# One front stage for modulation and norm, a deferred modulation on GpSimd, and decay and gate rows over 128 partitions

## What is computed

```
m_lat = split(silu(c)     @ w_mod + b_mod, 6)     # shift1, scale1, gate1, shift2, scale2, gate2
m_ctx = split(silu(c_ctx) @ w_mod + b_mod, 6)     # of these only shift1, scale1 are used
h     = rms_norm(x, norm1_g) * (1 + scale1) + shift1      # latent and context tokens
p     = h @ w_in                                  # 4640 columns: q k v ga | 32 decay and gate columns | hq hff hfb hv gb
log_g = -exp(a_log) * softplus(p_a + dt_bias);  beta = sigmoid(p_b)      # from the 32 columns
... two scans (gated delta rule, HGRN2), each forward and backward, w_out ...
x     = x + gate1 * y
x     = x + gate2 * mlp(rms_norm(x, norm2_g) * (1 + scale2) + shift2)
```

## Time and profile before

| | us |
|---|---|
| median of three runs | 4352.18 |
| the profiled execution, its own time | 4353.56 |
| its span, first to last instruction | 4351.8 |
| TensorE busy | 3614.9 |
| VectorE busy | 1880.8 |
| ScalarE busy | 1377.6 |
| POOL busy | 697.0 |
| mean granted TensorE clock | 0.907 |

### The profile page before, as it was taken

How to read it: one execution, slowest core, us unless ns; L and a number is a source line. 1 busy time by engine, 2 the same in 40 slices (tenths; PEclk the granted TensorE clock), 3 DMA queues, 4 the chain that set the end, 5 groups by cost and what they waited for, 6 DMA issues and landing times. The chain is left out here.

```text
span 4351.8 us, 98698 instructions
## 1 busy us (share of the span) xinstructions
PE 3614.9 (83%) x42292; PEld 2976.9 (68%) x42292; DVE 1880.8 (43%) x2660; ACT 1377.6 (32%) x1858; POOL 697.0 (16%) x752
## 2 busy tenths in 40 slices
PE   2549999999968888857674428899999888999998
PEld 2327788888857777747664227688888666888886
DVE  7647851111025555545546943523323335233233
ACT  0336641433125555513332212312212223122122
POOL 0000000000035555505556102000000220000002
PEclk9779999999979999966777668899999888999998
DMA  6412232243223333354442263111111231111111
GB/s 234 145 43 49 54 80 75 99 130 100 72 95 109 108 106 113 104 105 85 102 86 70 68 217 107 35 48 52 44 52 46 81 107 35 49 52 44 52 46 58
DMA packets 460370, 365.08 MB, mean 84 GB/s; under 512 B 115908, under 2 KB 413192, under 8 KB 454408
## 3 DMA queue, kind: packets, MB, share of 16 engines
q1 hardware_dynamic: 430088, 315.94, 25.2%
q0 software_dynamic: 6912, 25.17, 1.7%
q10 hardware_dynamic: 23168, 20.97, 1.6%
HBM read 262.64 MB, written 99.39 MB: 83 GB/s over the span
## 5 line engine op out<-in xcount | busy, mean ns | idle before, releaser
L2289 PE MATMUL o_pg<-o_h_hi,o_w_hi 128*128 128x512 f32 x1280 | 516.9, 404 | 70.6 <-DVE o_h_lo L2438 48.6
L527 PE MATMUL p_pg<-h_hi,p_whi 128*128 128x512 f32 (+3 forms) x1384 | 531.4, 384 | 25.5 <-DVE p_wlo L702 25.5
L527 PE MATMUL p_pg<-h_lo,p_whi 128*128 128x512 f32 (+3 forms) x1384 | 519.3, 375 | 0.0
L527 PE MATMUL p_pg<-h_hi,p_wlo 128*128 128x512 f32 (+3 forms) x1384 | 519.3, 375 | 0.0
L2290 PE MATMUL o_pg<-o_h_lo,o_w_hi 128*128 128x512 f32 x1280 | 509.1, 398 | 0.0
L2291 PE MATMUL o_pg<-o_h_hi,o_w_lo 128*128 128x512 f32 x1280 | 509.0, 398 | 0.0
L2289 PE MATMUL o_pg<-o_f_hi,o_w_hi 128*128 128x512 f32 x1024 | 398.3, 389 | 0.0
L2290 PE MATMUL o_pg<-o_f_lo,o_w_hi 128*128 128x512 f32 x1024 | 398.3, 389 | 0.0
L2291 PE MATMUL o_pg<-o_f_hi,o_w_lo 128*128 128x512 f32 x1024 | 398.3, 389 | 0.0
L2289 PEld LDWEIGHTS o_pg<-o_h_hi,o_w_hi 128*128 128x128 f32 x1280 | 245.6, 192 | 150.8 <-issue 46.9
L527 PEld LDWEIGHTS p_pg<-h_hi,p_whi 128*128 128x128 f32 (+1 forms) x1384 | 258.4, 187 | 81.5 <-DVE p_wlo L702 26.3
(11 more groups left out here) (279 smaller groups left out, 6265.6 us busy)
## 6 DMA issues: line engine op xcount, KB each, us to landing
o_raw<-in_w_mlp SPq DMA_DIRECT2D x128, 512.0 KB, 4.1
g_kqvb<-scr_kqv SPq DMA_DIRECT2D x72, 384.0 KB, 3.5
mod_w<-in_w_mod SPq DMA_DIRECT2D x6, 4096.0 KB, 13.1
p_raw<-in_w_in SPq DMA_DIRECT2D x38, 512.0 KB, 5.9
g_kqa<-scr_kqv SPq DMA_DIRECT2D x72, 256.0 KB, 3.0
scr_kqv<-p_y SPq DMA_DIRECT2D x24, 576.0 KB, 4.9
scr_hf<-p_y SPq DMA_DIRECT2D x16, 576.0 KB, 5.3
scr_hk<-p_s SPq DMA_DIRECT2D x16, 576.0 KB, 8.2
```

Source lines behind the costliest of these rows:

```text
L527: last = nc.tensor.matmul(pg[0:m, bank, 0:n], w[:, q, k, 0:m], h[:, k, hoff:hoff + n], start=(k == 0 and j == 0), stop=(k == KT - 1 and j ...
L2289: nc.tensor.matmul(out, w_hi[:, p, k, :], half(rhs[0], k, h), start=(k == 0), stop=False)
```

## The change

`phase_mod` and `phase_norm` become one `phase_front`, and parts of `phase_project` change.

- **Front.** Only the first 2048 of the 6144 columns of w_mod are used here, in eight slices of 1 MB (one per row group) through four slots. TensorE multiplies them directly, with silu(c) and silu(c_ctx) as two stationary columns (`products`); the result is two rows, turned by 16 small transposes. The small vectors are loaded from ScalarE's queue, decay constants from POOL's in 16 transfers.
- Squares are taken from the tokens before the transpose, per tile of 128 tokens with an accumulated sum: three tiles of a block on ScalarE, the fourth on VectorE. The sums are thus one number per partition; the reciprocal is of 128 x 4, becomes four diagonal matrices, and a matmul with ones spreads it (`spread`).
- The scaled row is one VectorE operation (gain and reciprocal root together), `h_hi` adds the shift on ScalarE, and `h_lo` is one VectorE operation (add the shift, subtract `h_hi`).
- Token loads, stores of xT (now from SP's queue) and the first two weight tiles of the projection stand in one written-out order; x has two buffers, some of the buffers lie in space of later `h` blocks. `h_hi` and `h_lo` are one tensor per block.
- **Projection.** The 32 decay and gate columns are repeated four times, so the result stands on 128 partitions; each 32 partitions keep one latent block and a quarter of the context (576 elements). All four rows live in `p_y1`. They are stored in 32 transfers; only tile 1 waits for them. No step in the scans' arithmetic changes.
- **Deferred modulation.** POOL multiplies and adds the other 4096 columns of w_mod in eight pieces of 512 columns, 64 slices of 256 KB that it loads itself, and TensorE sums each piece over the partitions after every fourth tile. `e.mod` and the last gain are finished at the end of the projection.

```
+def phase_front(nc, e):
...
+                for k in range(4):
+                    load_w(k)
+                load_x(0)
+                for k in range(4, KT):
+                    load_w(k)
+                load_x(1)
+                load_x(2)
+                sp.dma_start(e.p_raw[:, 0, :, 0:AB_W], e.w_in[0].rearrange("(k p) n -> p k n", p=P)[:, :, AB_COL:AB_COL + AB_W]
+                             ).then_inc(e.p_w_in[0], 16)
+                sp.dma_start(e.p_raw[:, 1], e.w_in[0].rearrange("(k p) n -> p k n", p=P)[:, :, 0:P]).then_inc(e.p_w_in[1], 16)
+                store(1)
+                load_x(3)
+                store(2)
+                load_x(4)
+                store(3)
+                store(4)
+                for i in range(3):
+                    sp.wait_ge(stored[i], 16 * len([q for q in range(2, 10) if q % 3 == i]))
...
+                def products(k):
+                    pe.wait_ge(wm_in[k % 4], 16 * (k // 4 + 1))
+                    for n in range(4):
+                        last = nc.tensor.matmul(mp[0:2, n, :], e.sc[:, k, :], wm[k % 4][:, n, :],
+                                                start=(k == 0), stop=(k == KT - 1))
+                    last.then_inc(wm_used, 1)
...
+                for b in range(1 + NB):
+                    for k in range(KT + 1):
+                        if k < KT:
+                            copy(b, k)
+                        if k >= 1:
+                            high(b, k - 1)
+                        if 1 <= b < NB and 3 <= k < 6:
+                            square(b + 1, k - 3)
+                        if 1 <= b < NB and k == 6:
+                            roots(b + 1)
...
+                    dve.scalar_tensor_tensor(ur[:, g % UR, 0:n], xt[:, g % RING, 0:n], e.gain[:, g0 + k:g0 + k + 1],
+                                             mp[:, b % 2, 0:n], ALU.mult, ALU.mult).then_inc(u_ready, 1)
...
+                    dve.scalar_tensor_tensor(e.h_lo[b][:, k, :], ur[:, g % UR, 0:n], e.mod[:, s0 + k:s0 + k + 1],
+                                             e.h_hi[b][:, k, :].bitcast(F32), ALU.add, ALU.subtract).then_inc(lo_ready, 1)
...
+                def mod_sums(c, released):
+                    pe.wait_ge(m_acc, c + 1)
+                    pe.wait_ge(group_free, released)
+                    for s in range(TB // P):
+                        last = nc.tensor.matmul(modps[:, c * 4 + s:c * 4 + s + 1], macc[:, s * P:(s + 1) * P],
+                                                e.ones[:, 0:1], start=True, stop=True)
+                    last.then_inc(m_sums, 1)
...
+                for x in range(MC * KT):
+                    c, k = divmod(x, KT)
+                    w = mw[:, x % 2]
+                    sc = e.sc[:, k, 0:1]
+                    pool.wait_ge(mw_in[x % 2], 16 * (x // 2 + 1))
+                    if k == 0:
+                        if c:
+                            pool.wait_ge(m_sums, c)
+                        nc.gpsimd.tensor_scalar(macc[:, :], w, sc, None, ALU.mult).then_inc(m_part, 1)
+                        done += 1
+                    else:
+                        nc.gpsimd.tensor_scalar(w, w, sc, None, ALU.mult).then_inc(m_part, 1)
+                        pool.wait_ge(m_part, done + 1)
+                        nc.gpsimd.tensor_tensor(macc[:, :], macc[:, :], w, ALU.add).then_inc(m_part, 1)
+                        done += 2
...
+                nc.scalar.activation(whi[:, 0].rearrange("p k (q r) -> p k q r", q=4),
+                                     raw[:, 0, :, 0:AB_W].unsqueeze(2).to_broadcast([P, KT, 4, AB_W]), ACT.Copy).then_inc(w_hi, 1)
...
+                        nc.scalar.activation(ab_g[r, to], src, ACT.Identity, bias=e.dtb[r, :])
+                        last = nc.scalar.activation(ab_y[r, to], src, ACT.Sigmoid)
...
-                        if m < 2:
-                            act.wait_ge(ab_out, 16 * 6)
-                        else:
+                        if m == 1:
+                            act.wait_ge(ab_out, 16 * 32)
+                        elif m:
...
-                dve.wait_ge(ab_out, 16 * 3)
-                dve.tensor_tensor_scan(yrow[0][0:AB_W, :], m, g, 0.0, ALU.mult, ALU.add).then_inc(ab_d, 1)
+                dve.tensor_tensor_scan(ab_c, m, g, 0.0, ALU.mult, ALU.add).then_inc(ab_d, 1)
```

More of the change, by code:

```diff
@@ L128, in _ @@
+            @block.scalar
+            def _(act):
                 v = [(V_BMOD, 48, e.b_mod[0].rearrange("(r n) -> r n", n=P)),
@@ L140, in _ @@
[L140 to L149, removed]
@@ new lines, in high @@
+                def high(b, k):
+                    g = 8 * b + k
+                    nt, g0, s0 = BLOCKS[b]
+                    act.wait_ge(u_ready, g + 1)
+                    nc.scalar.activation(e.h_hi[b][:, k, :], ur[:, g % UR, 0:nt * P], ACT.Identity,
+                                         bias=e.mod[:, s0 + k:s0 + k + 1]).then_inc(hi_ready, 1)
+                for a in range(2):
+                    square(0, a)
+                roots(0)
+                for a in range(3):
+                    square(1, a)
@@ new lines, in inverse @@
+                def inverse(b):
+                    t, n = T0[b], BLOCKS[b][0]
+                    dve.wait_ge(root, b + 1)
+                    dve.reciprocal(rs[:, t:t + n], rs[:, t:t + n]).then_inc(inv, 1)
+                    dve.wait_ge(inv, b + 1)
+                    if b:
+                        dve.wait_ge(bc_ready, b)
+                    for a in range(n):
+                        last = dve.tensor_scalar(diag[:, a, :], e.ident, rs[:, t + a:t + a + 1], None, ALU.mult)
+                    last.then_inc(diag_ready, 1)
@@ new lines, in _ @@
+                dve.tensor_copy(mrow[:, 2:4, :], mp[0:2, 2:4, :]).then_inc(mrow_dve, 1)
+                dve.wait_ge(mod_turned, 1)
+                m = cc[:, C_MOD:C_MOD + 32].rearrange("p (s a) -> p a s", a=2)
+                bm = e.cols[:, V_BMOD:V_BMOD + 16]
+                dve.tensor_tensor(e.mod[:, 0:16], m[:, 0, :], bm, ALU.add).then_inc(chain, 1)
+                dve.tensor_tensor(e.mod[:, 48:64], m[:, 1, :], bm, ALU.add).then_inc(chain, 1)
+                dve.wait_ge(chain, 7)
+                for j, sc0 in enumerate((8, 56)):
+                    last = dve.scalar_tensor_tensor(e.gain[:, 8 * j:8 * j + 8], e.mod[:, sc0:sc0 + 8], 1.0,
+                                                    e.cols[:, V_G1:V_G1 + 8], ALU.add, ALU.mult)
@@ new lines, in _ @@
+                last.then_inc(mod_ready, 1)
+                dve.wait_ge(mod_ready, 1)
+                for b in range(1 + NB):
+                    for k in range(KT + 1):
+                        if k < KT:
+                            scale(b, k)
+                        if k >= 1:
+                            low(b, k - 1)
+                        if b == 0 and k == 2:
+                            inverse(1)
+                        if 1 <= b < NB and k == 4:
+                            square(b + 1)
+                        if 1 <= b < NB and k == 7:
+                            inverse(b + 1)
@@ L400, in phase_project @@
         pgf = pg[:, :, :].rearrange("p b t -> p (b t)")
+        AL = TB + CTX // 4
+        ab_y, ab_g, ab_m, ab_c = (yrow[1][:, x * AL:(x + 1) * AL] for x in range(4))
         def group_no(m, j):
@@ L484, in store @@
+                load(0)
+                sp.wait_ge(ab_a, 5)
+                for d in range(2):
+                    store_ab(e.sbeta[d], 16 + 8 * d, ab_y, d)
+                sp.wait_ge(ab_d, 6)
+                store_ab(e.sgam[0], 0, ab_c, 0)
+                sp.wait_ge(ab_d, 9)
+                store_ab(e.sgam[1], 8, ab_g, 1)
                 def store(m):
```

478 lines of the change are left out of this document (251 added, 227 removed).

## The result

| | before | after |
|---|---|---|
| median of the runs beside each other, us | 4355.73 | 4186.98 |
| lowest to highest of four | 4346.83 to 4361.99 | 4185.07 to 4188.69 |
| ratio after to before, 95% interval | | 0.9614, 0.9594 to 0.9633 |
| span of the profiled execution, us | 4351.8 | 4183.2 |

The change gives 168.7 us, and 168.6 between the two profiled spans.

A forecast was written before the change was run, and what follows sets the result against it. TensorE matmuls bound most of the kernel (83% busy), but not its first 345 us. Gains of 140.8 (front) and 18.8 (decay rows), less 14.3 and 2, made 143.3 off 4353.6, then 1.4 less: 4209 us, range 4193 to 4232.

The forecast's parts named there:

- Shift and gain at 40.3: New front: products to 34.8 us, then copies, small transposes and VectorE's sums, so shift and gain stand at 40.3 us.
- 2 us, twice: Front's latent blocks: ScalarE, and VectorE behind it, wait 2 us twice for token tiles queued behind stores; 112.6 becomes 116.6.
- Rival A: Front: transfers set its length, ScalarE's squares waiting 8 us in three blocks and a late last store; +20, 4229; chance 0.15.
- Rival D: Front: steps at the engines' floor, 1.25 us each, and no transfer wait; -13, 4196; chance 0.12.
- First sums at P+41.9 and idle 6: Projection: first sums of squares 41.9 us after its first matmul, against 60.7 before, TensorE idle 6 before them; 18.8 gained.
- Rival E: Decay rows: the hole in the projection stays, as the 128-partition chain or its many stores take as long; 4228; chance 0.02.
- 1.78 per piece, 14.3 lost: Deferred modulation in the projection: TensorE's fp32 column sums cost 1.78 us for each of eight pieces, 14.3 us lost.
- I give the products 2.4 GHz: Start of the front: modulation products run at 2.4 GHz, 32 x 0.86 = 27.5 us; a slow start would cost 2 us.
- Rival C: Front: modulation products run at 1.2 GHz throughout; +27, 4236; chance 0.05.
- VectorE beside POOL, 2 us: Projection: POOL's deferred modulation lengthens VectorE operations with SBUF inputs; between 0 and 7.8 us, taken as 2 lost.
- Rival B: Projection: POOL's collisions reach further, stretching 39 normalising multiplications after 345 us by 0.4 and splits as much; +18, 4227; chance 0.07.
- rival F: Projection: TensorE waits every four tiles for POOL's piece; slower than before, 4414 at 17 us a slice; chance 0.01.

## Why the prediction was wrong, and where it was right

The order of things came as forecast: the front gives nearly everything, the decay rows 19, the deferred sums take a little back, nothing else moves. Nearly all the errors went the same way, so together they left the range.

- **The front, 122.5 forecast and 111.69 measured.** Shift and gain at 40.3: 40.34. In it two errors cancel. The products ran to 37.26 and not 34.8, for the most part because TensorE started at 1.2 GHz (2.2 of the 2.5); the 16 small transposes took 1.1 us and not 3.5. I priced them by a row that differs twice: it turned 128 columns where these have two, and its stretch, 165 to 169 us, has a granted clock of 0.57. Then the context block took 8.2 (9.7 forecast), the three blocks 47.6 (49.5), the last 11.6 (11.6). Inside a block errors cancel as well. In block 2, five plain steps took 6.7 (7.25 forecast) and the three with squares 6.0 (7.2), but the change to the next block took 3.3 and not 2.0, as these two scalings show, 4.63 apart of which 1.3 is the step:

```profile
75.56 0.74 DVE L398 SCALAR_TENSOR_TENSOR n_u<-n_xt,gain,n_mp 128x512 f32<-128x512 f32 x1
80.19 0.75 DVE L398 SCALAR_TENSOR_TENSOR n_u<-n_xt,gain,n_mp 128x512 f32<-128x512 f32 x1 [1.56 <-issue]
```

So the nearness of 15.9 to 16.5 is in part luck. The failed step is the next: "2 us, twice" for token tiles behind the stores. There is no such wait, since ScalarE wants the tile 8.9 us after the last copy and not 5.5; it takes twice the stores to make VectorE wait 1.4 and 0.6. Nor is there the 1.5 for filling and draining. The last store cost 1.5 beyond the last low part and not 3; cast, split and hand-overs 2.4 and not 2.9. In sum 1.5 + 1.9 + 4 + 1.5 + 1.5 + 0.5 = 10.9. Rival A, which had transfers set the front, falls: even the double stores cost the blocks only 1.0. Rival D, steps at the floor without transfer waits, was the closest of all with 4196; it had the missing waits right, while its 1.25 a step was 1.32.
- **The decay rows.** First sums at P+41.9 and idle 6: P+41.75 and 5.96. Its steps came out too: Ln ends at P+33.5 (33.5 forecast), the second scan at P+38.8 (38.7), the convolution at P+40.8 (40.9). Two of its parts, the length of the passes and the wait for stores, are measured as 11 and 6.7 of 17.7 at G. Rival E falls.
- **The column sums: the step that failed worst.** "1.78 per piece, 14.3 lost": they take 0.81 in place and cost 5.5 at G, within the 2 us to which the marks repeat. The row was taken as one at 2.4 GHz, for its stretch is recorded at 1.00. It ran at 1.2 GHz, and awake it is 1.84 per 16 instructions. I had the counter-evidence and did not apply it: the forecast names the granted clock of 0.50 after an idle front and still gives this term no lower bound. Halving it alone would have put the forecast at 4202.
- **The clock.** "I give the products 2.4 GHz" was wrong. The Trainium skill (TensorE: Matmul & The Clock Gate, What's actually happening), which I set aside because the record did not agree, has an idle array at 1.2 GHz by default. The pace of the instructions agrees with the page, 0.86 against 0.43 us, and so do both kernels with TensorE kept awake. By the page I expected the products to be 2 us worse, and they are 2.2 worse (9.26 us against 7.03). It bore more on two prices where I did not think of it, the rows for the column sums and for the small transposes. Rival C, 1.2 GHz throughout, falls: from 11.87 us on the products run at twice the pace.
- **VectorE beside POOL, 2 us.** Measured 0.9 at G and 1.1 to 2.5 from P to G, with the loads in it; the term may have been right. The collisions lengthen a split by a tenth and a normalising multiplication by 49 ns. The Trainium skill (SBUF — State Buffer, Who interferes with whom) is not contradicted in kind, as VectorE's operations do get longer; of the up to 7.8 us that the forecast allowed for by it, a third at most appeared. Rival B falls. Its price was also wrongly added: by its own words it is 39 times 0.4, which is 15.6, and as much again, 31 and not 18, and that would have lain outside the range. A slice takes 3.9 us and not 3, as a multiply by a scalar takes 1.57 and not between 0.62 and 1.30. That costs nothing, as POOL waits 54 to 126 us for TensorE ahead of each further piece; rival F is far.
- **The rest unchanged**: right, once two executions of each are averaged. But an execution's scan phases vary by more than 10 us, and I gave the range no part for it.

What stays open: why the stores land so fast. The row that frightened me, 13.3 us for a 2 MB store beside a 2 MB load, was a store in one piece; here halves of 1 MB took 4.4 us in the median. Whether the smaller pieces or the missing neighbour made them faster was not tried. Nor is it known why equal code from P to G differs by up to 2.2 us.

## What to carry to other kernels

A price from a trace holds at the clock at which its row ran, and the recorded clock alone did not tell that here: look at the pace of two equal instructions, early and late, before a row from an idle stretch prices work in a busy one. Give every term an end on the cheap side too; several terms, each sized a little on the dear side, made an error of 20 us together. And where runs spread by more than an edit is worth, read the edit at a mark right behind the last stage that it can touch, and learn from all executions with equal code how well that mark itself repeats.

## What was not expected of the hardware

- The granted clock is recorded as 1.00 from the start of an execution, while TensorE's first work runs at half the pace of its later work: products 0.86 us apart up to 11.28, 0.43 after; 16 column sums in 3.57 us cold and 1.84 awake, both at a recorded 1.00.
- GpSimd multiplies 128x512 elements by a scalar in 1.57 us and adds two such tensors in 1.28: the operation with one tensor is the slower.
- GpSimd's work beside VectorE's splits lengthened them from 1225 to 1344 ns, and reached the end of the projection as about 1 to 2.5 us of 951, hardly more than equal code differs.
- The same instructions from G to the end took between 3112 and 3137 us in thirteen profiled executions of kernels that are equal there, while from P to G equal code repeated within 2.2 us.
